# Overflow item moved to the middle of the expert pairs, and output weights fetched ahead for a first tile that takes both halves row by row

## The reference

```python
n1  = rmsnorm(x, g_mix)
mix = mixers(n1)                    # gated delta rule (4 heads of 128) | causal convolutions, 1024 wide
h   = x + mix @ w_out               # 1024 x 1024
xn  = rmsnorm(h, g_moe)
# hierarchical router: 8 groups of 8 experts, best group, best 2 experts in it
y   = sum over the 2 experts e of a token: gate * ((silu(a) * b) @ w_down[e]),  a, b = split(xn @ w_up[e])
h   = h + y                         # w_up[e] 1024 x 512, w_down[e] 256 x 1024, 64 experts
h   = h + sigmoid(rmsnorm(h, g_ple) @ w_ple_gate) * (p @ w_ple_proj)
out = rmsnorm(h, g_final)
```

## Time and profile before

| | |
|---|---|
| Time, median of 3 runs | 1468.87 us (1466.95, 1468.87, 1472.25) |
| Profiled execution: time, span | 1466.72 us, 1465.0 us |
| Mean granted TensorE clock | 0.902 |
| Busy: PE, DVE, ACT, POOL | 1191.1, 630.3, 320.4, 243.2 us |
| HBM read and written | 264.12 MB, 25.43 MB |
| up weights: transfers, time to landing | 64 of 2048 KB, median 16.9 us |

### The profile page before, as it was taken

How to read it: one execution, slowest core, us unless ns; L and a number is a source line. 1 busy time by engine, 2 the same in 40 slices (tenths; PEclk the granted TensorE clock), 3 DMA queues, 4 the chain that set the end, 5 groups by cost and what they waited for, 6 DMA issues and landing times. The chain is left out here.

```text
span 1465.0 us, 16352 instructions
## 1 busy us (share of the span) xinstructions
PE 1191.1 (81%) x5812; PEld 796.7 (54%) x5812; DVE 630.3 (43%) x859; ACT 320.4 (22%) x667; POOL 243.2 (17%) x340
## 2 busy tenths in 40 slices
PE   4999999997688877799409987888788887748997
PEld 3888888885577776688303332233333232216775
DVE  7399989873466453432461111111111111135553
ACT  5221221214344423322101110000101010032222
POOL 2100000003545651000011211111112111011111
PEclk9999999967699998799659998899999999978999
DMA  4212121100000000521567799999999999952321
GB/s 146 59 43 57 43 57 43 29 1 0 1 1 1 1 1 14 182 86 72 208 253 312 317 425 426 428 422 409 413 402 417 421 410 401 397 205 82 120 94 43
DMA packets 68052, 272.57 MB, mean 186 GB/s; under 512 B 11625, under 2 KB 38442, under 8 KB 51370
## 3 DMA queue, kind: packets, MB, share of 16 engines
q1 hardware_dynamic: 56096, 254.30, 43.8%
q0 software_dynamic: 9456, 16.80, 3.0%
q10 hardware_dynamic: 2458, 0.92, 0.3%
HBM read 264.12 MB, written 25.43 MB: 198 GB/s over the span
## 5 line engine op out<-in xcount | busy, mean ns | idle before, releaser
L2080 PE MATMUL ps_u<-wup,xgT 128*64 128x512 f32 x1024 | 263.8, 674 | 67.5 <-DMA wup<-in_w_up_dram 65.1
L2080 PEld LDWEIGHTS ps_u<-wup,xgT 128*64 128x64 f32 x1024 | 85.9, 155 | 244.1 <-issue 242.9
L92 PE MATMUL ps_b<-n_hi,wh 128*128 128x512 f32 x384 | 150.5, 392 | 6.1 <-DVEq L405 6.1
L92 PE MATMUL ps_b<-n_lo,wh 128*128 128x512 f32 x384 | 150.3, 391 | 0.0
L92 PE MATMUL ps_b<-n_hi,wl 128*128 128x512 f32 x384 | 150.2, 391 | 0.0
L2003 DVE TENSOR_TENSOR hb<-sil,ps_u 128x256 f32<-128x256 f32 x32 | 13.5, 421 | 308.5 <-ACT sil L1943 308.5
L92 PEld LDWEIGHTS ps_b<-n_hi,wh 128*128 128x128 f32 x384 | 72.7, 189 | 21.5 <-ACTq L40 6.5
L92 PEld LDWEIGHTS ps_b<-n_hi,wl 128*128 128x128 f32 x384 | 72.6, 189 | 15.3
L92 PEld LDWEIGHTS ps_b<-n_lo,wh 128*128 128x128 f32 x384 | 72.6, 189 | 15.2
L1943 ACT ACTIVATE sil<-ps_u 128x256 f32<-128x256 f32 x32 | 12.3, 384 | 296.2 <-PE ps_u L2080 296.2
L423 DVE SCALAR_TENSOR_TENSOR convT<-upad,vecT,convT 128x1024 f32 (+1 forms) x60 | 76.8, 1281 | 0.0
(11 more groups left out here) (369 smaller groups left out, 2069.7 us busy)
## 6 DMA issues: line engine op xcount, KB each, us to landing
wup<-in_w_up_dram SPq DMA_DIRECT2D x64, 2048.0 KB, 16.9
zT<-in_w_down_dram SPq DMA_DIRECT2D x32, 1024.0 KB, 17.0
convT<-in_w_down_dram SPq DMA_DIRECT2D x32, 1024.0 KB, 19.0
wraw<-in_w_in_dram SPq DMA_DIRECT2D x25, 512.0 KB, 4.0
convT<-y_rows SPq DMA_DIRECT2D x16, 512.0 KB, 5.3
qkvT<-in_x_dram SPq DMA_DIRECT2D x8, 512.0 KB, 7.6
qkvT<-in_w_out_dram SPq DMA_DIRECT2D x8, 512.0 KB, 5.2
xr<-in_x_dram SPq DMA_DIRECT2D x8, 512.0 KB, 3.3
```

Source lines behind the costliest of these rows:

```text
L92: ins = nc.tensor.matmul(ps, lhs[a], rhs[b], start=first and k == 0, stop=last and k == 2)
L2080: last = nc.tensor.matmul(ps_u[k][HC[c], :], xgT[k][:, j, HC[c]], wup[k][c][:, j, :], start=j == 0, stop=j == NJ - 1)
```

## The change

SP fetches the first four blocks of `w_out` in the delta rule's block, once ACT has read the values of the last pair. In the output projection SP fetches only blocks 4 to 7. PE takes the first tile with a function of its own, `out_both`, which goes through the weight blocks once and does both halves with each; the wait for the router weights is moved to the first router product.

In the experts' block the pair loops are cut in two at `MID` = 8, that is behind pair 15. The overflow items stand between the two loops on PE, ACT, DVE and POOL. SP fetches the weights of the first item ahead of its loop as before, and those of further ones between its two loops.

```diff
+        NWO = 4
+        s_wo = [sem(f"s_wo{s}") for s in range(NWO)]
+        wo_raw = [qkvT[:, NT + s, :] for s in range(NWO)]
...
+            @blk.sync
+            def _(sp):
+                sp.wait_ge(*a_one.sem_at("silv1", NP2 - 1))
+                for j in range(NWO):
+                    sp.dma_start(wo_raw[j], w_out[0, j * P:(j + 1) * P, :]).then_inc(s_wo[j], 16)
...
-                for j in range(NJ):
-                    if j >= NWO:
-                        sp.wait_ge(s_wo_lo, j - NWO + 1)
+                for j in range(NWO, NJ):
+                    sp.wait_ge(s_wo_lo, j - NWO + 1)
                     sp.dma_start(wo_raw[j % NWO], w_out[0, j * P:(j + 1) * P, :]).then_inc(s_wo[j % NWO], 16)
...
-                        if early(t, 1) and h == 0:
-                            pe.wait_ge(s_wo_lo, j + 1)
...
+                def out_both():
+                    for j in range(NJ):
+                        pe.wait_ge(s_wo_lo, j + 1)
+                        for h in range(2):
+                            last = mm3(ps_o[:, h, :], [mix[0][0][:, j, :], mix[0][1][:, j, :]],
+                                       [wo[0][:, j, HF[h]], wo[1][:, j, HF[h]]], j == 0, j == NJ - 1)
+                            if j == NJ - 1:
+                                last.then_inc((o_o0, o_o1)[h], 1)
...
-                pe.wait_ge(s_wr, 32)
...
+            MID = NIT // 2
...
+                with sp.If(n_over > 0):
+                    fetch_over(0)
+                fetch_pairs(0, MID)
+                with sp.If(n_over > 1):
+                    with sp.Fori(1, n_over) as v:
+                        fetch_over(v)
+                fetch_pairs(MID, NIT - 1)
...
                 pool.wait_ge(s_clear, NS + 1)
                 over_tokens(0)
-                for k in range(NS):
-                    turn(1, k)
+                with pool.Fori(1, MID + 1) as i:
+                    for k in range(NS):
+                        turn(i, k)
...
-                with pool.Fori(2, NIT) as i:
+                with pool.Fori(MID + 1, NIT) as i:
...
                 for k in range(NS):
                     pair(0, k)
+                with pe.Fori(1, MID) as i:
+                    for k in range(NS):
+                        pair(i, k)
                 n_over = pe.value_load(nov[0:1, 0:1], min_val=0, max_val=NOV)
                 with pe.If(n_over > 0):
                     with pe.Fori(0, n_over) as v:
                         over(v)
-                with pe.Fori(1, NIT - 1) as i:
+                with pe.Fori(MID, NIT - 1) as i:
```

More of the change, by code:

```diff
@@ L1348, in hybrid_block_kernel @@
         o_xn, o_T, o_xT, o_r, o_lg = (sem("out_" + n) for n in ("xn", "T", "xT", "r", "lg"))
-        NWO = 4
-        s_wo = [sem(f"s_wo{s}") for s in range(NWO)]
         s_wo_hi, s_wo_lo = sem("s_wo_hi"), sem("s_wo_lo")
@@ L1358, in hybrid_block_kernel @@
             wo = [sb(f"wo_{n}", [P, NJ, D], F32R, c5) for n in ("hi", "lo")]
-            wo_raw = [qkvT[:, NT + s, :] for s in range(NWO)]
             mix = [[sb(f"mix_{n}{g}", [P, NJ, P], F32R, c5) for n in ("hi", "lo")] for g in G2]
@@ L1515, in routers @@
                     pe.wait_ge(o_xT, t + 1)
-                    if not early(t, 1):
+                    if early(t, 1):
+                        pe.wait_ge(s_wr, 32)
+                    else:
                         pe.wait_ge(o_lg, t)
@@ L1841, in _, with fetch_over, fetch_pairs @@
             def _(sp):
+                def fetch_over(v):
+                    e = sp.value_load(eov[0:1, ds(v, 1)], min_val=0, max_val=NE - 1)
+                    wait_alone(sp, s_od, v + 1)
+                    sp.dma_start(wup_x[:], up_p[:, ds(e, 1), :, :]).then_inc(s_oup, 16)
+                    sp.dma_start(wdn_x[:], dn_p[:, ds(e, 1), :, :]).then_inc(s_odn, 16)
+                def fetch_pairs(first_, last_):
+                    with sp.Fori(first_, last_) as i:
+                        for k in range(NS):
+                            p = NS * i + k
+                            wait_alone(sp, s_u, p + 1)
+                            for c in G2:
+                                fetch_up(sp, k, c, ds(p + NS + NPR * c, 1))
+                            wait_alone(sp, s_d, p + 1)
+                            for c in G2:
+                                fetch_down(sp, k, c, ds(p + NS + NPR * c, 1))
                 n_over = sp.value_load(nov[0:1, 0:1], min_val=0, max_val=NOV)
@@ L1964, in _ @@
                     pair(0, k)
+                with act.Fori(1, MID) as i:
+                    for k in range(NS):
+                        pair(i, k)
                 n_over = act.value_load(nov[0:1, 0:1], min_val=0, max_val=NOV)
@@ L2031, in _ @@
                     pair(0, k)
+                with dve.Fori(1, MID) as i:
+                    for k in range(NS):
+                        pair(i, k)
                 n_over = dve.value_load(nov[0:1, 0:1], min_val=0, max_val=NOV)
@@ L2042, in _ @@
                         nc.vector.tensor_copy(ye_x[:, HF[1]], ps_y[HC[0], 1, :]).then_inc(s_oy1, 1)
-                with dve.Fori(1, NIT - 1) as i:
+                with dve.Fori(MID, NIT - 1) as i:
                     for k in range(NS):
```

32 lines of the change are left out of this document (10 added, 22 removed).

## The result

The changed kernel takes **1458.65 us** (median of 10 runs, 1452.24 to 1462.92); the kernel before, on the same chip, 1468.59 us (10 runs, 1464.86 to 1473.62). The ratio is 0.993, with a 95% interval of 0.9911 to 0.9948: 10 us less, between 8 and 13. That is inside the range of the prediction and on its side, 3.7 us above its number.

What follows compares the result with a forecast made beforehand. No single resource bounds the span: TensorE in the output projection, DMA engines in the experts. 1466.7 - 5.9 - 7.0 = 1453.8 us, raised about half way towards the runs' median to 1455.0 us; range 1450 to 1461.

Steps and rivals of the forecast that it cites:

- Term 1, the first tile: Output projection: early weight blocks let TensorE start at 588.7 and the second tile at about 602.9 against 608.8; -5.9 us.
- The rise of the granted clock, the rival with 0.07: Output projection's first tile: clock stays down, all 48 matmuls at 0.43 us, first gain lost; 1460.9 us, chance 0.07.
- The waits costed at nothing: Delta rule's early fetch, router weights' wait, pair 18's gather and cut loops: each costed at 0 us.
- The router weights' wait and the cut loops: Wait moved to the first router product, one more loop per engine in the experts: each cost 0 us.
- The gather: Experts, behind the item: pair 18's gather may come up to 7.4 us late; costed at 0, 2 kept for the range.
- Term 2, the item: Experts: moving the overflow item behind pair 15 removes 8.3 us of idle DMA and adds 1.3; -7.0 us.
- The queue is thus full for 27.5 us behind an up product: Experts, behind pair 15: the next request comes after 28.85 us, so the DMA queue runs dry for 1.3 us.
- a window of 3 us under 0.5: Experts, behind the item: a DMA share under 0.5 for 3 us would show the prediction wrong.
- the queue runs as dry in the middle as at the start: Experts: the item only moves and its gain of 7.0 us is gone; 1462.0 us, chance 0.06.
- a dear gather: Experts: pair 18's gather comes 7.4 us late, 3 to 4 us of idle DMA return; 1458.5 us, chance 0.07.
- a slower kernel: Experts: the gather lands some 33 us behind its issue instead of 13.9; 1473.5 us and above, chance 0.02.
- the share can't be 1 from the first ring fetch on: Experts: DMA share forecast at 1 from the first ring fetch, no window below 0.9 before the item.

Runs made afterwards that it cites:

- e5: Kernel before with only the early fetch of four projection weight blocks; projection stage 128.2 us against 131.0, total time -2.1 to +2.5 us against the kernel before.
- e9: Changed kernel with GpSimd issuing pair 18's gather ahead of the overflow item's scatter; 1459.55 us.
- e3: Kernel before with the overflow item's up product made twice, behind pair 1; experts stretch 446.6 us against 438.5 for its like.
- e4: Changed kernel with the overflow item's up product made twice, behind pair 15; experts stretch 437.5 us against 433.3 for its like.
- e2: Kernel before with only the overflow item moved behind pair 15, projection as before; -3.5 us against the kernel before, between -6.5 and -0.6.
- e7: Changed kernel with the overflow item behind pair 7 instead of pair 15; 1457.5 us.
- e10: Changed kernel with the overflow item split: up product behind pair 15, down product behind pair 16; 1455.1 us.
- e11: Changed kernel with the overflow item split and placed behind pair 7, its down product one pair later; 1456.0 us.
- e12: Changed kernel with the overflow item back at its old place but split: up product behind pair 1, down product behind pair 2; 1462.66 us.
- e6: Kernel before with both halves row by row and the router wait moved, no early fetch; projection stage 127.1 us against 131.0, total -5.3 to 0 us.

## Why the prediction was right, and where its steps were off

**Term 1, the first tile: right, -5.9 forecast and -6.1 measured** (P of 124.9 in the eight other executions with all three edits, against 131.0 over the three old ones; in the profiled one the gain is 7.3). Step by step: TensorE started at 588.31 for a forecast 588.7, released by block 0 as said. Block 4 was fetched in 3.3 us (588.19 to 591.49) and not in the 5.8 that I took from a queue of eight, so it was there 3 us early; the three behind it lost most of that again, for they came at intervals of up to 2.4 us and not of 1.27. The low part of block 7 was ready at 599.73 (forecast 600.6). The second tile began 18.8 us behind the block's start; the forecast said 19.5, and the eight others have 19.3 to 19.5. One step of the sum has a slip that hardly counts: 602.6 less 0.7 is 601.9, not 602.1, so by its own numbers the term is -6.1. The rise of the granted clock, the rival with 0.07, came 5.5 to 5.9 us behind the first matmul in the eight others (forecast 5.9) and 3.3 behind it in the profiled one:

```profile
588.00:591.00 3.00, 2.69 (x6) 2.15 (x7) 3.00 (x4) 1.49 (x2) 0.00 (x0) 0.50 0.60 188
591.00:592.00 1.00, 1.00 (x5) 0.81 (x4) 0.57 (x1) 0.51 (x1) 0.00 (x0) 0.72 0.84 197
592.00:602.00 10.00, 9.52 (x41) 7.25 (x40) 7.14 (x8) 4.78 (x6) 0.00 (x0) 1.00 0.65 240
```

From 592 on it stays at the 2.4 GHz level, although TensorE changes the half of `ps_o` with every third matmul. The Trainium skill, TensorE: Matmul & The Clock Gate, "A second HAM failure mode: psum-queue depth-cycling", tells of a kernel whose clock went up and down while it cycled through PSUM banks; the page puts that down to frequent short idles of TensorE between groups of matmuls. In this tile TensorE idles once, for 0.2 us, so changing halves alone does not bring the clock down here, and the page's own case is not tested.

**The waits costed at nothing: right.** From ScalarE's last read of the values to the output projection there are 73.9 to 80.6 us in the ten kernels that fetch ahead and 74.1 to 78.2 in the four that don't: no cost of the fetch is seen, but one of 2 or 3 us would not be either, and e5's total is where one could hide. The router weights' wait and the cut loops show in no stage length. The gather was 2.1 us late, inside the bound of 7.4, and e9 shows it to be free.

**Term 2, the item: right in sign and mechanism, -7.0 forecast, -5.2 in E and -6.0 in X measured.** By E the item cost 438.5 - 430.9 = 7.6 us behind pair 1, where the forecast saw 8.3 in idle transfers, and 433.3 - 430.9 = 2.4 behind pair 15, where it saw 1.3. Both are within 1.1 us. But the step that led to the 1.3 was wrong: "The queue is thus full for 27.5 us behind an up product". I took the time at which the last byte of pair 16's up weights landed, 22.5 us behind their issue, for the time until which all engines are busy. What was there to move was 8.0 MB, 18.8 us at 425 GB/s, and most engines stood dry from about 1031 on. I had named that as a sign of being wrong (a window of 3 us under 0.5), and there are four. That the time came out near nevertheless is luck as far as the working goes. It rests on a second fact that I did not know: in this stretch most of such dry time costs nothing. What counts more is when the last part of what is queued has landed, and for that the 27.5 is nearly right: in the changed kernel the last part of pair 17's down weights landed at 1041.8, 28.9 us behind the issue at 1012.85.

The reading that fits is this. A transfer is done when the last of its 16 parts has landed, and the weights of a product, two transfers of one semaphore, when the last of 32 has. The Trainium skill says so too: DMA: Bandwidth & Descriptors, "Why a DMA increments its semaphore by 16 and not by 1", has the engines of one transfer finish independently, with a count for each. The trace records a time for each count, and they show the lag. Early, all engines are level: of the 32 counts of pair 3's up weights before, the last 16 came between 805.6 and 808.3. Later they are not: of pair 16's before, the 24th came at 1025.1 and the last at 1033.9, and TensorE began at 1033.98; of pair 17's in the changed kernel the 17th came at 1025.3 and the last at 1036.8. So the share is 1.0 for all in the steady stretch, but a few engines lag, and it is for these that TensorE waits. When the item stops the requests, the ones ahead run dry first, and a tail of 0.1 to 0.3, two to five engines of 16 by share, goes on for 8 to 10 us. From the last count of the down weights queued there to the next issue of up weights there are, in us:

```
                          e3     before  e4    e9    changed  e2     e7     e10    e11    e12
last count to next issue  12.5   5.9     5.7   1.1   0.1      -0.2   -0.2   -5.0   -5.9   -0.9
E above 430.9             15.7   7.4     6.6   2.3   2.6      2.3    1.8    0.1    -0.7   6.8
```

Where it is long the item is dear, and where the last part lands well behind the next issue the item costs nothing. All but some 1 to 3 us of what a whole item costs is this dry time of the last engine; e12, behind pair 1, is the exception. The mean share orders them less well: idle of 5.1, 10.3 and 15.4 us in the middle (e10, the changed kernel, e4) goes with 0.1, 2.6 and 6.6 above an E without an item, and 8.5 behind pair 1 with 7.4. That the last 16 of 32 counts are spread over up to 11.5 us is shown; which engine makes the last one the trace doesn't name, why the lag builds up no run tests, and what the remaining 1 to 3 us are stays open.

The named rivals: that the queue runs as dry in the middle as at the start was right about the queue (10.3 us of idle against 8.5) and wrong about the time. The clock staying down, a dear gather, and a slower kernel did not come. One slip of names in the prediction: the issue at 1011.44 is the one behind pair 14's up product, for pair 16's weights, and the product that waited for them is pair 16's. The interval of 22.5 us between them stands, but by the same slip the item was forecast at 1003 to 1019 and stood one pair later, at 1018.4 to 1034.5. One more sign was put wrongly: the share can't be 1 from the first ring fetch on, for both ring slots are filled before the pairs begin (share 0.28 from 735 to 750). From 780 to 1012 it is.

**The sum.** 5.9 + 7.0 = 12.9 was forecast. P gives 6.1 and E and X give 5.2 to 6.0, that is 11 to 12. The stretch between them takes some 0.7 back (64.6 us in the mean of the nine kernels with all three edits of the projection, 63.9 over the three with none), which is less than the scatter of those three, 63.3 to 65.1. The medians give 9.9 with an interval of 8 to 13. The median lies 3.7 us above my number: 3.0 of it are the sum (12.9 against 9.9), 0.7 the reference, which I had put at 1467.9 and ten runs put at 1468.6.

## What to carry to other kernels

Where transfers set the pace, time taken on a compute engine is cheap exactly there: put odd pieces of work where that engine already waits, not at the stretch's head, where it doesn't yet; and cut the piece in two if it holds back the requests for longer than the queue is deep (that took another 2.3 us off E here, which the total time can't confirm). A queue has two depths: bytes queued over the rate says when most engines run dry, the landing of the last part says when the last one does, and what counts for the time is nearer to the second. A mean share is not a cost: 8.5 us of idle went with a cost of 7.6 in one place, 10.3 us with 2.4 in another, so price a hole by lengthening or shortening it. And for gains of a few microseconds compare the lengths of the touched stages between fixed events, and then look for the same gain in the total: e5's 2.8 us, read from one stage, were not found there.

## What the runs showed of the hardware

- A queue that is kept full by one program drains unevenly: behind pair 15 the share goes 1.00, 0.61, 0.27, 0.17, 0.18, 0.13, 0.05 in windows of 2 us, behind pair 1 0.87, 0.14, 0.06, 0.00. From pair 7 on, the later the place, the fewer bytes are moved in the gap of a whole item: 10.1, 8.0 and 7.4 MB behind pairs 7, 15 and 27. The last 16 of the 32 counts of the up weights queued there come within 2.7 us behind pair 1, 7.5 behind pair 7, 11.5 behind pair 15 and 11.2 behind pair 27.
- After such a hole the engines are back at once: the share in the 2 us from the next issue on is 0.72 behind pair 15 and 0.86 behind pair 1, so no more than 0.6 us are lost. The 2.0 us of fixed cost that the prediction cited from the Trainium skill, DMA: Bandwidth & Descriptors, "Anatomy of one DMA", do not come on top. The page's figure is for transfers issued from GpSimd, and these are issued from SyncE; it puts most of the 2.0 us into the confirmation of the last byte, which would agree.
- With the same code up to there, the granted clock rose from 1.2 to 2.4 GHz at two different times behind the output projection's first matmul: 3.3 us in the changed kernel against 5.5 to 5.9 in its eight like, and 3.0 in e3 against 6.0 in the kernel before and e2. e6, alone of its kind, has 3.7, and e5 5.5. In the changed kernel's first tile the early rise goes with 0.6 us; the other 0.9 us by which P of that execution is shorter than its like were not traced. No run tells what decides it.
- The start of the output projection scatters over 10 us between executions, and it comes from the delta rule: ScalarE's first read of `qkvT` there is at 364.6 to 366.9 us in all of them, and from it to the output projection there are 214.7 to 225.0 us (214.7 and 223.6 in two kernels whose delta rule is the old one). Its cause is not known.
